# A two-block model on one Trainium2 core: the first layer's norm moved behind its products, and the a_qk convolution split between two engines

## The reference, cut to what matters

```python
h = rmsnorm(x, norm_mix_g[0])          # x * rs * g, rs = 1/sqrt(mean(x^2) + eps) of each row of x
proj = h @ a_w_in                      # queries and keys qk, values v, output gate o, 8 gates, q_mem
qk = silu(causal_dwconv(qk, a_conv_w, a_conv_b))   # 4 taps along the 256 rows
gates = gates + a_gate_b               # input gate, log forget gate
hm = mlstm_chunkwise(q, k, v, ig, log_sigmoid(fg))
mem_out = memory_attention(q_mem, mem, mem_w_kv[0])
x = x + concat([head_norm(hm) * sigmoid(o), mem_out]) @ a_w_out
x = x + conv_ffn(rmsnorm(x, norm_ffn_g[0]), ...)
k, v = split(rmsnorm(x, kv_norm_g) @ w_kv)         # for the band attention of layer 1
```

## Time and profile before

| | |
|---|---|
| median of three runs | 1407.7 us (1406.91 to 1407.94) |
| profiled execution | 1407.12 us |
| its span in the trace | 1405.3 us |
| TensorE busy | 1378.3 us (98%) |
| VectorE busy | 1109.1 us (79%) |
| ScalarE busy | 758.1 us (54%) |
| TensorE's mean granted clock | 0.999 |

### The profile page before, as it was taken

The page is one execution under the profiler, slowest core; times in us unless marked ns, Lnnn a source line. Parts: engine busy times, 40 slices in busy tenths (PEclk is TensorE's granted clock), DMA queues, the critical chain, the costliest instruction groups (busy, mean ns, idle before and its releaser), DMA issues.

```text
span 1405.3 us, 25320 instructions
## 1 busy us (share of the span) xinstructions
PE 1378.3 (98%) x9708; PEld 1233.6 (88%) x9708; DVE 1109.1 (79%) x1709; ACT 758.1 (54%) x1037; POOL 36.0 (3%) x38
## 2 busy tenths in 40 slices
PE   8999999999999999999999999999999999999997
PEld 8897989999988889999899897889999889888886
DVE  6897788888866788888876965588888768777776
ACT  6545555555655555555567644565555544545443
POOL 0001300000000000000000000100000000100000
PEclk9999999999999999999999999999999999999999
DMA  8436747767453347766622241367667655645550
GB/s 320 160 124 238 303 159 256 247 255 246 154 207 128 135 172 256 248 252 236 246 79 78 90 170 56 121 249 259 241 244 254 231 202 191 267 183 184 204 180 30
DMA packets 39402, 276.00 MB, mean 196 GB/s; under 512 B 4496, under 2 KB 4624, under 8 KB 6672
## 3 DMA queue, kind: packets, MB, share of 16 engines
q1 hardware_dynamic: 38016, 266.35, 51.9%
q0 software_dynamic: 1008, 7.86, 1.5%
q10 hardware_dynamic: 288, 0.52, 0.1%
HBM read 273.67 MB, written 1.05 MB: 195 GB/s over the span
## 4 chain that ended last, share of the span: by engine, by line
PE 81%; DVE 12%; ACT 4%; issue 2%; DMA 1%; SPq 0%; DVEq 0%; POOL 0%; ACTq 0%
PE L L2145 20%; PE D L2105 17%; PE L L2336 15%; PE L L2342 8%; PE N L2336 5%; DVE wlo L1156 4%; PE D L2725 3%; PE N L2342 3%; ACT whi L590 2%; PE D L2727 1%; PE D L2265 1%; PE D L2296 1%; DVE arena L1253 1%; PE D L2336 1%; PE N L2285 1%
## 5 line engine op out<-in xcount | busy, mean ns | idle before, releaser
L1156 DVE TENSOR_TENSOR wlo<-raw,whi 128x2048 fp32r<-128x2048 f32 x106 | 242.4, 2288 | 52.8 <-ACT whi L590 52.7
L2336 PE MATMUL L<-h_all,whi 128*128 128x512 f32 x960 | 240.9, 393 | 1.7 <-issue 1.7
L1342 DVE TENSOR_TENSOR wlo<-raw,whi 128x2048 fp32r<-128x2048 f32 x96 | 219.5, 2286 | 28.7 <-ACT whi L720 28.7
L590 ACT ACTIVATE whi<-raw 128x2048 fp32r<-128x2048 f32 x106 | 202.2, 1909 | 59.9 <-PE L L2145 43.1
L2145 PE MATMUL L<-h_all,whi 128*128 128x256 f32 (+1 forms) x992 | 206.5, 306 | 4.0 <-DVE h_all L1235 1.5
L2336 PEld LDWEIGHTS L<-h_all,whi 128*128 128x128 f32 x960 | 173.4, 189 | 33.5 <-issue 2.0
L720 ACT ACTIVATE whi<-raw 128x2048 fp32r<-128x2048 f32 x96 | 183.0, 1907 | 18.6 <-PE L L2342 18.6
L2145 PEld LDWEIGHTS L<-h_all,whi 128*128 128x128 f32 x992 | 160.5, 192 | 15.3 <-issue 7.0
L2145 PE MATMUL L<-h_all,wlo 128*128 128x256 f32 (+1 forms) x496 | 147.5, 301 | 0.0
L2342 PEld LDWEIGHTS L<-h_all,wlo 128*128 128x128 f32 x960 | 130.7, 190 | 9.2
L2105 PE MATMUL D<-hd_hi,whi 128*128 128x256 f32 x480 | 136.0, 283 | 0.8 <-DVE arena L1381 0.8
(11 more groups left out here) (388 smaller groups left out, 2508.5 us busy)
## 6 DMA issues: line engine op xcount, KB each, us to landing
raw<-in_units SPq DMA_DIRECT2D x250, 1024.0 KB, 4.8
arena<-in_band POOLq DMA_DIRECT2D x1, 2304.0 KB, 9.6
arena<-in_nax POOLq DMA_DIRECT2D x1, 1536.0 KB, 6.9
raw<-in_units SPq DMA_DIRECT2D x4, 256.0 KB, 5.3
x<-in_x SPq DMA_DIRECT2D x1, 1024.0 KB, 8.2
t<-in_ctx POOLq DMA_DIRECT2D x1, 1024.0 KB, 5.1
arena<-in_ctx POOLq DMA_DIRECT2D x1, 1024.0 KB, 5.0
out<-t SPq DMA_DIRECT2D x4, 256.0 KB, 2.1
```

What stands on the lines that cost most here:

```text
L590: A.activation(whi[weight_slot(v)][:], raw[v % RING][:], ACT.Copy).then_inc(unit_hi, 1)
L1156: V.tensor_tensor(wlo[w][:], raw[v % RING][:], whi[w][:].bitcast(FP), ALU.subtract) \
L1342: V.tensor_tensor(wlo[w][:], raw[v % RING][:], whi[w][:].bitcast(FP), ALU.subtract) \
L2336: mm(bank[:], w[0][:, k, part * P:part * P + P], h_all[:, k, 0:512], start=k == 0, stop=False, skip_group_check=True)
```

## The change

**Layer 0's rows.** h_all is made straight from x * g, without rs (`rows_hi` on ACT, `rows_lo` on DVE), as soon as g has arrived. `apply` and t are gone here. The factor rs now comes in where banks are evacuated: a_qm, a_v (through rs_col, rs turned into columns by two one-column products of PE, `scale_columns`), a_qk, a_o and the gate rows. The gate products read x, with their weights multiplied by g on DVE. mv0's unit is made in four pieces as well, and mk0's bank is evacuated ahead of them.

**The a_qk jobs.** DVE copies the bank, scaled by rs, to SBUF (`qk_scaled`, y_qk) and hands it back. ACT does the first tap with the bias (`first_tap_qk`, two Identity activations of 128x256). DVE does the other three taps from SBUF (`qk_taps`), behind a wait for ACT (qk_first), and ACT's silu waits for them (qk_taps). `gate_scans` stands behind the taps of the first of the four jobs.

**The try beside.** ctx_moment stands in slot 12 of layer 1's attention (T_B), the root at the start of ffn1. H_EARLY has PE do the first one, two and one blocks of a job's eight (3 matmuls of 512 columns each) ahead of the wait for hg_kdt in steps 5, 6 and 7 of the recurrence. T_N waits for the values at tile 4 alone. The first half row of the output is multiplied by the weight on POOL and by its root on ACT.

```diff
+H_EARLY = {5: 1, 6: 2, 7: 1}
...
-        shared = JOBS["e_nv1"][0].banked % 2
-        T_N[0]["needs"], T_N[3 - shared]["needs"], T_N[2 + shared]["needs"] = "e_nq", "e_nv0", "e_nv1"
+        T_N[0]["needs"], T_N[4]["needs"] = "e_nq", "e_nv1"
...
+                    sp.wait_ge(R["first_out"], 2)
+                else:
+                    sp.wait_ge(R["t_done"], KB * N_FINAL + n)
...
+            gp.wait_ge(R["x_ready"], 4 * 3 + 1)
+            gp.wait_ge(ld["finw"], 16)
+            nc.gpsimd.tensor_tensor(t_rows[:, 0, 0:512], xt[:, 0, 0:512], final_rows[:, 0:512], ALU.mult)                 .then_inc(R["first_out"], 1)
...
+            act.wait_ge(raw_full[1], 16)
+            for i in range(4):
+                c = slice(512 * i, 512 * i + 512)
+                A.activation(whi[1][:, c], raw[1][:, c], ACT.Copy).then_inc(R["piece_hi"] if i < 3 else unit_hi, 1)
+            made[0] = 2
+            act.wait_ge(R["ones_set"], 1)
+            A.activation(h_rs[:, 0, 0:1], ones[:, 0:1], ACT.Sqrt)
             upto(2)
             root()
+            act.wait_ge(ld["vec"], 16)
+            for i in range(4):
+                rows_hi(lambda k: vc("mix_g", k), i)
             upto(3)
-            apply()
...
+            def first_tap_qk(n):
+                at = VECS["a_conv"][0] + 10 * n
+                for c in range(2):
+                    w = at + 5 * c
+                    A.activation(m_y[n % 2][:, c, :], y_qk[n % 2][:, c, :], ACT.Identity, scale=vec[:, w:w + 1],
+                                 bias=vec[:, w + 4:w + 5]).then_inc(R["qk_first"], 1)
+
             def q_silu(n, j):
+                act.wait_ge(R["qk_taps"], n + 1)
                 dst = (aq if n < 3 else ak)[:, 2 * (n % 3):2 * (n % 3) + 2, :]
                 A.activation(dst, m_y[n % 2], ACT.Silu).then_inc(R["q_silu"], 1)
...
+                first_tap_qk(0)
...
+            def second_silu():
+                first_tap_qk(1)
+                q_silu(1, None)
...
+                first_tap_qk(n + 2)
...
-            act.wait_ge(R["cx_rv"], 1)
-            A.activation(rs2, rs2, ACT.Sqrt).then_inc(R["cx_rs"], 1)
...
+            act.wait_ge(R["first_out"], 1)
+            act.wait_ge(R["fin_rs"], 1)
+            A.activation(t_rows[:, 0, 0:512], t_rows[:, 0, 0:512], ACT.Identity, scale=h_rs[:, 0, 0:1]) \
+                .then_inc(R["first_out"], 1)
...
+            mk0 = JOBS["mk0"][0]
+            dve.wait_ge(job_done, mk0.number + 1)
+            to_mkv(0, 0)(0, mk0, bank(mk0)).then_inc(job_evac, 1)
+            for i in range(3):
+                values_piece(i)
             stat()
-            jobs("mk0", to_mkv(0, 0))
+            values_piece(3)
+            made[0] = 2
+            upto(2)
             dve.wait_ge(ld["vec"], 16)
-            apply(lambda k: vc("mix_g", k))
+            for i in range(4):
+                rows_lo(lambda k: vc("mix_g", k), i)
+            dve.wait_ge(ld["gate"], 16)
+            V.tensor_tensor(gw[:], gw[:], vc("mix_g", 0, KB).unsqueeze(2).to_broadcast([P, KB, 8]), ALU.mult) \
+                .then_inc(R["gate_w"], 1)
+            upto(3)
...
+            def qk_scaled(n, b):
+                if n > 1:
+                    dve.wait_ge(R["qk_taps"], n - 1)
+                return V.tensor_tensor(y_qk[n % 2], pair(b[:]), over_rows(rs[:]), ALU.mult)
+
+            def qk_taps(n):
+
+                at, y, src = VECS["a_conv"][0] + 10 * n, m_y[n % 2], y_qk[n % 2]
+                dve.wait_ge(job_evac, qk_job(n).banked + 1)
+                dve.wait_ge(R["qk_first"], 2 * n + 2)
+                for o in (1, 2, 3):
+                    for c in range(2):
+                        ins = V.scalar_tensor_tensor(y[:, c, o:T], src[:, c, 0:T - o], vec[:, at + 5 * c + o:at + 5 * c + o + 1],
+                                                     y[:, c, o:T], ALU.mult, ALU.add)
+                        if o == 3 and c == 1:
+                            ins.then_inc(R["qk_taps"], 1)
+                        else:
+                            step(ins)
+                    if o < 3:
+                        sync()
...
+                scale = rs[0:4].unsqueeze(1).to_broadcast([4, 2, T])
+                step(V.tensor_tensor(g_row[0:4, 0:2, :], M0[0:4, :].rearrange("p (a b) -> p a b", b=T), scale, ALU.mult))
...
-            jobs("a_qm", lambda n, j, b: V.tensor_scalar(qm, pair(b[:]), 0.125, None, ALU.mult))
+            jobs("a_qm", lambda n, j, b: V.scalar_tensor_tensor(qm, pair(b[:]), 0.125, over_rows(rs[:]), ALU.mult, ALU.mult))
             step(V.memset(v_one, 1.0))
+            dve.wait_ge(R["rs_turn"], 1)
+            step(V.tensor_copy(rs_col[:], Dn[2][:, 0:2]))
+            sync()
...
+                    dst = av[:, :, 256 * n:256 * n + 256]
+                    for tb in range(2):
+                        ins = V.tensor_scalar(dst[:, tb, :], b[:, tb * T:tb * T + T], rs_col[:, tb:tb + 1], None, ALU.mult)
+                        if n % 2 == 0 or tb == 0:
+                            step(ins)
                     if n % 2 == 0:
                         half = P if n == 0 else 0
-                        step(V.tensor_copy(v_halves(n), pair(b[:])[:, :, half:half + P].rearrange("p s (c m) -> p s c m", m=64)))
-                    return V.tensor_copy(av[:, :, 256 * n:256 * n + 256], pair(b[:]))
+                        sync()
+                        ins = V.tensor_copy(v_halves(n), dst[:, :, half:half + P].rearrange("p s (c m) -> p s c m", m=64))
+                    return ins
...
-            attention(T_A, 0, 0, 0, NARROW, BESIDE_A, stores, {2: gate_copy, 5: gate_rows})
-            gate_scans()
-            jobs("a_qk", lambda n, j, b: qk_conv(n + 2, j, b), {2: gate_columns}, rest_behind=(3,))
+            stores.update({JOBS[f"a_qk{n}"][0]: (lambda b, n=n: qk_scaled(n, b)) for n in range(2)})
+            attention(T_A, 0, 0, 0, NARROW, BESIDE_A, stores,
+                      {2: gate_copy, 5: gate_rows, 7: lambda: qk_taps(0), 9: lambda: qk_taps(1)})
+            def behind_taps(n):
+                def run():
+                    qk_taps(n + 2)
+                    if n == 0:
+                        gate_scans()
+                    if n == 2:
+                        gate_columns()
+                return run
+
+            jobs("a_qk", lambda n, j, b: qk_scaled(n + 2, b), {n: behind_taps(n) for n in range(4)}, rest_behind=(3,))
...
-                V.tensor_copy(ao[:, 2 * n:2 * n + 2, :], pair(bank(j)[:])).then_inc(job_evac, 1)
+                V.tensor_tensor(ao[:, 2 * n:2 * n + 2, :], pair(bank(j)[:]), over_rows(rs[:]), ALU.mult).then_inc(job_evac, 1)
...
-                tail=ctx_moment)
...
+            between[12] = ctx_moment
...
-                row_scale(0)
+                row_scale(1)
                 row_moment(1)
-                for n in (1, 2, 3):
+                for n in (2, 3):
...
+            def values_ready(k):
+
+                if k < 6:
+                    pe.wait_ge(R["piece_lo"], k // 2 + 4)
+                else:
+                    pe.wait_ge(*used(1))
+
+            job(JOBS["mv0"][0], True, ready=values_ready)
...
+            def scale_columns():
+                pe.wait_ge(R["rs_done"], stats[0])
+                for tb in range(2):
+                    ins = mm(Dn[2][:, tb:tb + 1], rs[0:1, tb * P:tb * P + P], ones[0:1, 0:1], start=True, stop=True)
+                ins.then_inc(R["rs_turn"], 1)
...
+                if e in H_EARLY:
...
+                    job(H_BESIDE[e][-1], True, order=range(H_EARLY[e]), end=False)
...
+                    job(H_BESIDE[e][-1], True, order=range(H_EARLY[e], KB), begin=False)
```

More of the change, by code:

```diff
@@ L867, in _ @@
             attention(T_A, 0, 0, NARROW, BESIDE_A,
-                      {JOBS["a_qk0"][0]: first_silu, JOBS["a_qk1"][0]: lambda: q_silu(1, None)}, {6: forget_logs})
+                      {JOBS["a_qk0"][0]: first_silu, JOBS["a_qk1"][0]: second_silu}, {6: forget_logs})
             def a_keys(n, j):
+                first_tap_qk(n + 2)
                 q_silu(n + 2, j)
@@ L969, in _ @@
             root()
+            act.wait_ge(R["cx_rv"], 1)
+            A.activation(rs2, rs2, ACT.Sqrt).then_inc(R["cx_rs"], 1)
             act.wait_ge(R["mod_ready"], 1)
@@ L1602, in _ @@
             stores = {JOBS[f"a_v{n}"][0]: store_av(n) for n in range(3)}
-            stores.update({JOBS[f"a_qk{n}"][0]: (lambda b, n=n: qk_conv(n, None, b)) for n in range(2)})
-            attention(T_A, 0, 0, 0, NARROW, BESIDE_A, stores, {2: gate_copy, 5: gate_rows})
-            gate_scans()
-            jobs("a_qk", lambda n, j, b: qk_conv(n + 2, j, b), {2: gate_columns}, rest_behind=(3,))
+            stores.update({JOBS[f"a_qk{n}"][0]: (lambda b, n=n: qk_scaled(n, b)) for n in range(2)})
@@ L1722, in _ @@
             V.memset(rs2, 0.0).then_inc(R["cx_fold"], 1)
-            ffn("ffn0", 0, CAUSAL3, scaled=False, g=lambda k: vc("kv_g", k), each_block=(ctx_add, lambda k, b: None),
-                tail=ctx_moment)
```

(24 more changed lines are left out.)

37 lines of the change are left out of this document (21 added, 16 removed).

## The result

The changed kernel takes 1417.14 us (median of 4 runs, 1417.10 to 1418.54) against 1407.82 us (4 runs, 1406.91 to 1408.16): a ratio of 1.0070 (95% interval 1.0059 to 1.0082). That is 9.3 us slower. The forecast was slower by 6.6 us, 1413.7, with a range to 1416.5; the time lies 0.6 us outside it. The profiled execution took 1417.11 us, with a span of 1415.2 us, 9.9 more than before.

A forecast was written before the change was run, and what follows sets the result against it. TensorE, busy 98%, was taken as the bound, with DVE's chain ending alongside PE's in the a_qk stretch. 6.4 + 1.5 + 1.2 - 1.6 - 0.95 + 0 = +6.55 on 1407.12 gave 1413.7 us, range 1411.5 to 1416.5.

The forecast's parts named there:

- The worse end of the chances: Whole kernel: two slow clock stretches or first taps later still, 1417 us, chance 0.05.
- The term of the scores: Layer 0's a_qk stretch: DVE's longer chain makes the first scores late, +6.4 us after taking off overlaps from +7.0.
- PE's lead at a_qk0: Start of layer 0: of 1.8 to 2.4 us gained by PE, 0.9 is left at a_qk0; bounds 0 and 2.4.
- the waits for the first tap in the four jobs: DVE's a_qk chain: waits for ACT's first tap, sum 4.3 us, bounds 0 and 5.5, the third job's 2.3.
- The term of the clock: PE's idle stretch of some 7 us before the scores: clock falls to half, +1.5 us, bounds 0 and 3.
- The order of the scans and the low part: DVE's a_qk chain: 1.5 us of waiting where scans were; four low parts, not three, before the last tap, 2.2 each.
- ctx_moment: Slot 12 of T_B: stands ahead of the maxima and division, PE's transposes wait, +1.2 us, bounds 0.6 and 2.4.
- H_EARLY and T_N: Matmuls ahead of the hg_kdt waits: -1.6 us, up to -1.85; T_N's wait for the values goes: -0.95 us.
- The tail: End of kernel: one scaled half row less on DVE against POOL's contention, 0 us, bounds -0.7 and +0.7.
- The clock doesn't fall: Rival, PE before the scores: same path, idle stretch broken up or too short, 1412.2 us, chance 0.2.
- ACT keeps up: Rival, a_qk jobs: the 4.3 us of waits for first taps go, clock stays, 1407.9 us, chance 0.15.
- PE is the bound and the bank waits decide: Rival, layer 0: PE's lead survives, DVE's chain ends before a_o[0], waits of 0.4 and 0.66 go, 1403.8 us, chance 0.1.

The follow-up runs named there:

- The filler: The changed kernel plus 54 matmuls of 256 columns, result unread, on PE before the wait for the last silu: 1414.03 us, ratio 1.0045.
- the try beside alone: Kernel of before with only ctx_moment's move, H_EARLY, T_N's waits and the output's first half row on POOL and ACT: 1404.97 us, ratio 0.9982.

## Why the prediction was wrong, point by point

**The mechanism was right, two of its terms too small.** The forecast had +6.4 for the scores and +1.5 for the clock. They are 8.7 and 3.56. Together 4.35 us were missing; 1.0 came back elsewhere (-2.35 instead of -1.35); the span's 9.9 stands against the sum's 6.55. The worse end of the chances, 1417 at 0.05, named later first taps and two slow stretches. Both are in the trace, but the slow stretch that costs time is one long one.

**The term of the scores.** Of the 2.3 us that it was short:
- 0.6 was my own subtraction. The chain was summed to 34.0 and to scores at 109.0, that is +7.0; I then took off 0.6 for overlapping ends. The durations had been read, nearly all, as steps from start to start and had the overlaps in them already. The chain measured 34.8.
- 0.9 is the start of the chain, 75.2 and not 74.3. In the memory attention too DVE waited for ACT's first taps, 2.73 and 1.23 us; I had left 0.9 of PE's lead at a_qk0, and PE instead waited 3.0 for ACT's copy (L706), which stands behind the silu that waits for those taps. The lead was gone before the four a_qk jobs: -2.5 at 35, -0.35 at 70.
- 0.6 is the waits for the first tap in the four jobs: 1.23, 1.23, 2.48 and 0, together 4.94, where I had 1.0, 1.0, 2.3 and 0. The two Identity take 1.09, inside my "1.0 to 1.2"; the other 0.14 of each 1.23 is the time from the end of DVE's copy to ACT's start and from ACT's end back to DVE, which I had not put in.
- 0.2 is the scaled copies: three of the four are followed by a wait and take their full 0.68, not 0.61. The way from the last tap over the silu to the scores (110.0 to 110.73) is as before and as forecast.

**The term of the clock.** The price was taken from the wrong row. I used the slow stretch at the start of the program, 3.35 us, whose matmuls follow each other at half the rate though the row itself reads 1.00; here PE worked for 8.6 us at 0.50, and lost 3.56. The bound of 3 "for two such stretches" was the same row twice, and so no bound. The filler shows 3.1 of it in the time. That the clock would fall was right, and so was the length of the wait (7 us forecast, 7.3 measured).

**The order of the scans and the low part**, terms of the chain, is confirmed, at 2.2 us in the time. With the first tap on DVE as well it is 3.5 (1412.85 to 1409.32), since without ACT no new wait takes the low part's place.

**ctx_moment** was put at +1.2 and costs nothing. I had it ahead of the maxima of tiles 16 and 17; the trace has it one pair of tiles earlier than I read from the slot number, at 436.11, where DVE's next work was not waited for:

```profile
433.31 2.29 DVE L1191 TENSOR_TENSOR wlo<-raw,whi 128x2048 fp32r<-128x2048 f32 x1
435.51 0.69 DVE L1834 SCALAR_TENSOR_TENSOR arena<-L,rs 128x512 f32<-128x512 f32 x1
436.11 0.41 DVE L1809 TENSOR_SCALAR arena<-M 128x256 f32<-128x256 f32 x1
436.56 1.75 DVE L1811 RECIPROCAL arena<-arena 128x256 f32<-128x256 f32 x1
```

**Not foreseen:** PE waits 1.0 instead of 0.3 for L1416 at 520 us, with an offset that grows by 0.65. It grows by 0.6 in every kernel with ACT's first tap behind the scaled copy, and by only 0.3 in all the others, the try beside alone among them. Why is not shown.

**H_EARLY and T_N** were forecast at -1.6 and -0.95. The offset falls by 1.94 in the recurrence (just beyond the bound of 1.85) and by 0.95 at 861. The first is more than the waits themselves, 1.2, and the size of what was forecast is right for both.

**The tail** was forecast at 0: the gain and POOL's cost even. The offset is +9.63 at PE's last matmul and 9.9 in the span, so the tail costs 0.3, inside the bounds. DVE beside POOL, and the same instruction after it:

```profile
1405.73 1.28 DVE L2159 TENSOR_TENSOR arena<-arena 128x512 f32<-128x512 f32 x1
...
1407.65 0.69 DVE L2159 TENSOR_TENSOR arena<-arena 128x512 f32<-128x512 f32 x1
```

0.6 us more beside POOL's product, which ran from 1405.17 for 1.29. It is what the earlier trace rows had shown (0.95 against 0.41). The Trainium skill (GPSIMD Engine Reference, section 8) states that GpSimd shares its SBUF interfaces with VectorE and that DVE instructions with two SBUF inputs contend with it. The trace agrees: both inputs of this instruction are in SBUF, and it took 1.28 against 0.69.

**The rivals.** "The clock doesn't fall" was wrong by the rows. "ACT keeps up" was wrong: five waits, three of them in the four jobs, the longest 2.48 behind the table load, as forecast. "PE is the bound and the bank waits decide" was wrong too, though it became true in the kernel with ACT's tap from the bank, whose DVE chain ends at 99.7: there the waits of 0.44 and 0.66 went, as that rival had it.

## What to carry to other kernels

Handing work to an idle engine helps only where its result is made while the first engine does something else: ACT's two Identity cost 4.3 us between a copy and the taps that need it (in six jobs), and brought 1.6 us (1404.97 to 1403.32) beside a low part (in four jobs, read from the bank, without the copy). Where two chains end together, a lead of one of them is worth nothing, and may turn into idle time in which TensorE's clock falls; price that fall by the work that follows at half the clock, not by the wait. And when a fill-in such as a scan is moved, ask what wait it had filled.
